# One of four low parts of each unit of the second expert table moves from VectorE to GpSimd, with four smaller edits

## The reference

```python
# 1. mixers: z = h @ w_in; windowed attention with sinks, gated; short convolution, gated; @ w_o; LN1
probs = softmax over a band of 128 keys and one sink          # 32 heads, 4 blocks of 128 tokens
h = layer_norm(ALPHA * h + mixed, ln1_g, ln1_b)
# 2. PEER: 8 heads x 16 chosen experts of 16384 for each token
u = take(u_tab, expert);  act = gelu(x . u);  wgt = gate * act
v = take(v_tab, expert);  y = sum over 128 slots of wgt * v
# 3. h = layer_norm(ALPHA * h + ffn, ln2_g, ln2_b)
```

## Time and profile before

| | us |
|---|---|
| median of 3 runs | 3801.84 (3796.93 to 3808.63) |
| the profiled execution's own time | 3810.41 |
| its span | 3808.6 |
| TensorE matmul busy | 3738.3 (98%) |
| VectorE busy | 2721.8 (71%) |
| ScalarE busy | 1394.6 (37%) |
| GpSimd busy | 1076.9 (28%) |

### The profile page before, as it was taken

One profiled execution on the slowest core, in us unless ns is written; L12 is line 12 of the kernel. 1 busy time (PEld: TensorE's weight loads), 2 busy tenths in 40 slices (PEclk: granted clock), 3 DMA queues, 4 the chain that ended last, 5 costly groups with the idle time before them and its releaser, 6 DMA issues.

```text
span 3808.6 us, 59840 instructions
## 1 busy us (share of the span) xinstructions
PE 3738.3 (98%) x24007; PEld 3431.3 (90%) x24007; DVE 2721.8 (71%) x3395; ACT 1394.6 (37%) x2023; POOL 1076.9 (28%) x579
## 2 busy tenths in 40 slices
PE   8999999999999999999999999999999999989998
PEld 8899999999977888888888899999999987878787
DVE  5644555456688765656556788888888877888888
ACT  5644444443425200000000144566665444434443
POOL 0000000000735433434444272232332212333432
PEclk9999999999999999999999999999999999999999
DMA  5345545554689999999999769999999989999996
GB/s 192 118 166 181 186 178 187 179 186 166 226 351 410 416 422 410 411 396 399 392 408 385 299 225 385 388 375 374 388 388 399 406 342 389 401 391 375 385 413 258
DMA packets 194970, 1232.67 MB, mean 324 GB/s; under 512 B 20144, under 2 KB 37120, under 8 KB 52736
## 3 DMA queue, kind: packets, MB, share of 16 engines
q1 hardware_dynamic: 109856, 656.51, 44.8%
q0 software_dynamic: 73728, 536.90, 34.6%
q10 hardware_dynamic: 11232, 37.23, 2.4%
HBM read 1193.34 MB, written 36.70 MB: 323 GB/s over the span
## 4 chain that ended last, share of the span: by engine, by line
PE 88%; DMA 5%; DVE 5%; ACT 1%; issue 1%; DVEq 0%; SPq 0%; ACTq 0%
PE dense_ps L1022 24%; PE dense_ps L1007 14%; PE dense_ps L1009 14%; PE dense_ps L1008 14%; PE dense_ps L1271 7%; PE score_ps L1271 4%; DMA wbuf<-in_peer_v_dram 3%; PE dense_ps L1050 3%; DMA wbuf<-in_w_units_dram 2%; PE oT_ps L1271 2%; PE o_ps L1271 2%; PE score_ps L1233 1%; PE score_ps L1123 1%; PE oT_ps L1163 1%; PE dense_ps L1145 1%
## 5 line engine op out<-in xcount | busy, mean ns | idle before, releaser
L1394 DVE TENSOR_TENSOR w_lo<-wbuf,w_hi_r 128x1024 fp32r<-128x1024 f32 x792 | 963.6, 1223 | 570.0 <-ACT w_hi_r L616 568.1
L616 ACT ACTIVATE w_hi_r<-wbuf 128x1024 fp32r<-128x1024 f32 x848 | 893.2, 1059 | 1118.6 <-PE dense_ps L1009 520.9
L1007 PE MATMUL dense_ps<-act_hi,w_hi_r 128*128 128x256 f32 x3968 | 1132.5, 285 | 3.1 <-DVE w_lo L1394 2.9
L1008 PE MATMUL dense_ps<-act_lo,w_hi_r 128*128 128x256 f32 x3968 | 1124.4, 283 | 0.0
L1009 PE MATMUL dense_ps<-act_hi,w_lo 128*128 128x256 f32 x3968 | 1124.2, 283 | 0.0
L1007 PEld LDWEIGHTS dense_ps<-act_hi,w_hi_r 128*128 128x128 f32 x3968 | 763.1, 192 | 15.4 <-issue 12.2
L1008 PEld LDWEIGHTS dense_ps<-act_lo,w_hi_r 128*128 128x128 f32 x3968 | 763.1, 192 | 0.0
L1009 PEld LDWEIGHTS dense_ps<-act_hi,w_lo 128*128 128x128 f32 x3968 | 762.8, 192 | 0.0
L1022 PE MATMUL dense_ps<-xT,wbuf 128*128 128x256 f32 x3136 | 687.2, 380 | 0.0
L1022 PEld LDWEIGHTS dense_ps<-xT,wbuf 128*128 128x128 f32 x3136 | 593.0, 190 | 91.0 <-issue 11.6
L562 POOL DMA_INDIRECT row<-in_peer_v_dram,expert x203 | 396.1, 1951 | 881.1 <-DVE h L1348 846.0
(11 more groups left out here) (292 smaller groups left out, 4294.9 us busy)
## 6 DMA issues: line engine op xcount, KB each, us to landing
wbuf<-in_w_units_dram SPq DMA_DIRECT2D x456, 1024.0 KB, 7.2
wbuf<-in_peer_v_dram SPq DMA_DIRECT2D x126, 1024.0 KB, 9.1
gate_spill<-gbuf ACTq DMA_DIRECT2D x8, 2048.0 KB, 12.0
e_gate<-gate_spill SPq DMA_DIRECT2D x32, 512.0 KB, 11.4
act_spill<-stage ACTq DMA_DIRECT2D x60, 256.0 KB, 9.2
e_act<-act_spill SPq DMA_DIRECT2D x30, 512.0 KB, 8.8
row<-in_peer_u_dram,expert POOLq DMA_INDIRECT x256, 14.2
row<-in_peer_v_dram,expert POOLq DMA_INDIRECT x203, 10.8
```

The costliest lines, as they stand in the source:

```text
L616: act.activation(hi_of(n)[j // 2][:, j % 2, :], w_of(n)[j // 2][:, j % 2, :], ACT.Copy).then_inc(w_hi_ready, 1)
L1007: nc.tensor.matmul(out, w[0], x[0], start=opens, stop=False)
L1008: nc.tensor.matmul(out, w[0], x[1], start=False, stop=False)
L1394: V.tensor_tensor(lo_of(n)[j // 2][:, j % 2, :], w_of(n)[j // 2][:, j % 2, :], hi_of(n)[j // 2][:, j % 2, :].bitcast(F32), ALU.subtract).t ...
```

## The change

It has five edits:

1. `by_pool` now also names quarter 1 of the units 4 to 59 of the V stage. So VectorE's list loses 56 low parts, and GpSimd's gets them. GpSimd's list for the V stage becomes a loop over units n: first all gathers with `FREE[g] <= ROWS_TO[n - 2]`, then `low(n, (1,))`.
2. In the U stage the gating of the one-hots comes before the high part (n+2, 2) rather than after it.
3. The weights of the final norm come in eight DMAs, of 512 columns each, over four pairs of units. For tile 0 the second step of the normalisation stays at unit 24 and the first goes to 23, the second residual split goes to 27, and the output is sent in four parts at units 26 to 29.
4. In half 1 the second group of five rows is spread: two ahead of the first softmax with the first five, one between `masks` and `denominators`, two after.
5. In half 0 the first `denominators` come ahead of the low parts (q0+2, 1) and (q0+2, 2).

```diff
-    return U_PQ < n < UNITS or UNITS + U_PQ + PLAIN_Q <= n < N_U + 4
+    return U_PQ < n < UNITS or UNITS + U_PQ + PLAIN_Q <= n < N_U + 4 or j == 1 and N_V + 4 <= n < N_V + 60
...
-            for g in range(ROWS_TO[N_U + 1] + 3, LATE_ROWS):
-                gather(g)
-            pool.wait_ge(dense_ready, N_V)
-            for g in range(LATE_ROWS, ALL_ROWS):
+            g = ROWS_TO[N_U + 1] + 3
+            for n in range(N_V + 4, N_V + 62):
+                while g < ALL_ROWS and FREE[g] <= ROWS_TO[n - 2]:
+                    if g == LATE_ROWS:
+                        pool.wait_ge(dense_ready, N_V)
+                    gather(g)
+                    g += 1
+                if n < N_V + 60:
+                    low(n, (1,))
+            for g in range(g, ALL_ROWS):
                 gather(g)
...
+                g = G_PER * (j + 1 - G_FIRST)
                 for k in range(3):
+                    if k == 2 and 0 <= g < HALF // 4:
+                        for r in range(G_PER):
+                            gate_rows(g + r)
                     split_hi(n + 2, k)
...
-STATS_AT, SD_AT, APPLY_AT, OUT_AT = (19, 61), (21, 61), (24, 62), (27, 62)
-RES_AT = (10, 24)
+STATS_AT, SD_AT, APPLY_AT = (19, 61), (21, 61), ((23, 24), (62, 62))
+OUT_AT = ((26, 27, 28, 29), (62, 62, 62, 62))
+RES_AT = (10, 27)
...
                 load(N_V + 2 + 2 * g)
                 load_e(3 + g)
+                if g == 0:
+                    sp.wait_ge(dense_ready, N_V)
+                load_ln2(0, g)
                 load(N_V + 3 + 2 * g)
-                if g % 2:
-                    sp.wait_ge(dense_ready, N_V)
-                    sp.dma_start(ln2[:, g // 2, :], ...).then_inc(ln2_in, 16)
+                load_ln2(1, g)
...
-                for n in range(n0, n0 + U_Q):
-                    rows(n)
+                rows(n0)
+                for p in range(2):
+                    rows(n0 + 1, p, 5)
...
                 masks(16 * b, 0, 0)
+                rows(n0 + 1, 2, 5)
+                denominators(16 * b)
+                for p in range(3, 5):
+                    rows(n0 + 1, p, 5)
                 split_lo(q0 + 2, 1)
                 split_lo(q0 + 2, 2)
-                denominators(16 * b)
```

More of the change, by code:

```diff
@@ L484, in load_act, with load_ln2 @@
                              act_spill[bass.ds(4 * i + q, 1), :, :].rearrange("o p x -> (o p) x")).then_inc(e_in[q % 2], 16)
+            def load_ln2(a, c):
+                part_c = slice(c * (D // 4), (c + 1) * (D // 4))
+                sp.dma_start(ln2[:, a, part_c], (ln2_b if a else ln2_g)[0, part_c].partition_broadcast(P)).then_inc(ln2_in, 16)
             def load_e(q, i=0):
@@ L511, in _ @@
                 load_e(3 + g)
+                if g == 0:
+                    sp.wait_ge(dense_ready, N_V)
+                load_ln2(0, g)
                 load(N_V + 3 + 2 * g)
-                if g % 2:
-                    sp.wait_ge(dense_ready, N_V)
-                    sp.dma_start(ln2[:, g // 2, :], (ln2_b if g // 2 else ln2_g)[0, :].partition_broadcast(P)).then_inc(ln2_in, 16)
+                load_ln2(1, g)
             with sp.Fori(0, GROUPS // 4 - 2) as i:
@@ L544, in _, with low @@
             pool.memset(mask[:, 0, 0:P], NEG).then_inc(masks_ok, 1)
-            def low(n):
-                for j in range(4):
+            def low(n, quarters=range(4)):
+                for j in quarters:
                     pool.wait_ge(w_hi_ready, HI[n, j])
@@ L633, in gathered_sd, with gathered_out @@
                 act.activation(sd2[:, :], mv2[:, 1:2], ACT.Sqrt, bias=eps[:, :]).then_inc(sd2_ready, 1)
-            def gathered_out(t):
+            def gathered_out(t, c):
+                part_c = slice(c * (D // 4), (c + 1) * (D // 4))
                 act.wait_ge(fin_step, 8 * (t + 1))
-                act.dma_start(out_v[:, t, :], h0[:, t, :]).then_inc(out_sent, 16)
+                act.dma_start(out_v[:, t, part_c], h0[:, t, part_c]).then_inc(out_sent, 16)
             def act_unit(j, placed=()):
@@ L948, in _ @@
                         gathered_sd(t)
-                    if m == OUT_AT[t]:
-                        gathered_out(t)
+                    for c in range(4):
+                        if m == OUT_AT[t][c]:
+                            gathered_out(t, c)
             for t in range(TILES):
@@ L958, in _ @@
                     act.dma_start(out_v[:, TILES + t, part_c], h1[:, t, part_c]).then_inc(out_sent, 16)
-            act.wait_ge(out_sent, 16 * (TILES + 2 * TILES))
+            act.wait_ge(out_sent, 16 * (4 * TILES + 2 * TILES))
         @block.tensor
@@ L1365, in finish_stats, with finish_apply @@
                 V.bn_aggr(mv2[:, :], bst2[:, :, :].rearrange("p c s -> p (c s)")).then_inc(fin_step, 1)
-            def finish_apply(t):
+            def finish_apply(t, second):
+                if second:
+                    dve.wait_ge(fin_step, 8 * t + 7)
+                    V.scalar_tensor_tensor(out=h0[:, t, :], in0=h0[:, t, :], scalar=rstd2[:, :], in1=ln2[:, 1, :],
+                                           op0=ALU.mult, op1=ALU.add).then_inc(fin_step, 1)
+                    return
                 dve.wait_ge(sd2_ready, t + 1)
@@ L1371, in finish_apply @@
                 dve.wait_ge(fin_step, 8 * t + 6)
-                dve.wait_ge(ln2_in, 32)
+                dve.wait_ge(ln2_in, 8 * 16)
                 V.scalar_tensor_tensor(out=h0[:, t, :], in0=h0[:, t, :], scalar=mv2[:, 0:1], in1=ln2[:, 0, :],
                                        op0=ALU.subtract, op1=ALU.mult).then_inc(fin_step, 1)
-                dve.wait_ge(fin_step, 8 * t + 7)
-                V.scalar_tensor_tensor(out=h0[:, t, :], in0=h0[:, t, :], scalar=rstd2[:, :], in1=ln2[:, 1, :],
-                                       op0=ALU.mult, op1=ALU.add).then_inc(fin_step, 1)
             for count in (masked, exp_done, pT_copied, aT_done, oT_ready, conv_step, gate_step, out_step,
@@ L1888, in _ @@
                         finish_stats(t)
-                    if m == APPLY_AT[t]:
-                        finish_apply(t)
+                    for second in range(2):
+                        if m == APPLY_AT[t][second]:
+                            finish_apply(t, second)
             for t in range(TILES):
```

## The result

| | before | after |
|---|---|---|
| median, us | 3799.39 (3796.90 to 3808.63, 4 runs) | 4059.05 (4051.01 to 4064.14, 4 runs) |
| ratio, 95% interval | | 1.0679 (1.0656 to 1.0703) |
| profiled execution, us | 3810.41 | 4061.67 |
| granted clock over the span | 0.992 | 0.969 |

The change makes the kernel 6.8% slower. The direction and the place were forecast; the size was not.

A forecast was written before the change was run, and what follows sets the result against it. TensorE, with matmuls in 98% of the span, was taken as the bound. 3810.4 + 407 (second table, units 5 to 59) + 3 (unit 7's gathers) - 18 (elsewhere) = 4202, stated as 4200; 8-in-10 range 4060 to 4255.

The forecast's parts named there:

- The chain: Second table: quarter 1 of unit n hangs through ScalarE, VectorE and GpSimd on quarter 2 of unit n-1; period 14.6 us.
- I take it that VectorE is first: Second table: VectorE's low part (n+1, 0) gets the ports before GpSimd's low part; period 18.9 us with the clock's loss.
- U + 11.34: End of GpSimd's low part if VectorE is first; U is when TensorE ends quarter 2 of unit n-1.
- the 2.24 that remain after VectorE's end: Earlier trace at 949.64: GpSimd's low part ended 2.24 us after VectorE's; taken to show reads later than its start.
- and through a series if there is no pause: GpSimd waits through VectorE's unbroken series; so held through low part (n+1, 0) and `e_mult` or `e_rest` to U + 9.10.
- The clock: Second table: TensorE returns at half clock after longer waits, losing 1.75 to 2.41, mean 2.1 us a unit, in quarter 1.
- the clock doesn't fall: Rival, regular waits in the second table: 4087 with VectorE first, 3966 with GpSimd first; chance 0.1 in its two forms.
- the 3.75 worked out for GpSimd first: TensorE's least wait ahead of quarter 1 in every unit: part ready at U + 9.19, needed at U + 5.44.
- The gains outside: Outside the second table: one-hots -9.2, first softmaxes -3.9 and -2.0, some 3 us of clock; -18 us.
- the right rival: GpSimd gets the ports first in the second table: period 16.7 us, +286, 4082; chance 0.2.
- Not slower: Rival, second table: gathers ahead don't wait for the last row; 3760 at best, some 3780 with DMA waits; chance 0.07.
- what would show it: Signs: one 5 to 6 us TensorE wait per unit before quarter 1, half clock behind each, DMA well under 0.98.

The follow-up runs named there:

- Taking it out by one index: Changed kernel with ROWS_TO[n - 3] for ROWS_TO[n - 2], so GpSimd's low part goes ahead of gathers waiting for section n-2: 3792.83 us, ratio 0.9984.
- shortening it by 1.08: Changed kernel with GpSimd making only the first 512 of 1024 columns of each moved low part, VectorE the rest: 3962.82 us, ratio 1.0420.
- the kernel with the rows early: Changed kernel with VectorE's rows of a second-table section put ahead of low part (n+2, 2) instead of after it: 3863.08 us, ratio 1.0159.
- the kernel with the pause: Changed kernel with a one-column memset on GpSimd, and a wait for it, between gathers and each moved low part: 4111.21 us, ratio 1.0819.
- an added wait: Changed kernel with GpSimd's low part of unit n waiting until VectorE has made low part (n+1, 0): 4212.85 us, ratio 1.1082.
- with the low part first: Changed kernel with each GpSimd low part ahead of the gathers that wait for section n-2, by ROWS_TO[n - 3]: 3792.83 us, ratio 0.9984.
- with quarter 3: Changed kernel with quarter 3 instead of quarter 1 on GpSimd, gathers still ahead of it: 3857.59 us, ratio 1.0162.
- without the move: Changed kernel with edit 1 undone, edits 2 to 5 kept: 3770.06 us, ratio 0.9937; once more 3769.56 us, ratio 0.9926.
- the kernel with the move alone: Kernel before with edit 1 alone: 4072.42 us, ratio 1.0729.
- half width: Changed kernel with GpSimd making 512 of the 1024 columns of each moved low part, VectorE the other 512: 3962.82 us, ratio 1.0420.

## Why the forecast was right, and where it failed

**The chain** was right. Each of its steps stands in one unit of the trace to 0.02 us up to GpSimd's start. Taking it out by one index gave back 266 of 289 us, shortening it by 1.08 gave back 96 (46 in waits and 45 in the clock, by its block), and taking the row from behind low part (n+2, 2) gave back 196, as expected.

**The step that failed** is the one put as "its first reads come later than its start, ... I take it that VectorE is first". It put GpSimd's low part at U + 11.34, and it ended at U + 9.10; that is 2.2 us a unit, the 121 us between 4202 and 4081. GpSimd was ahead of VectorE's low part (n+1, 0) in 53 of 55 units, in 46 of them against an earlier stamp. The rows behind that choice were of two kinds that don't bear on it: the earlier trace rows, where GpSimd's low part had no gather ahead of it, and the 2.24 that remain after VectorE's end. The stamps of the two starts were 0.01 to 0.04 apart in the 46, and they don't decide directly behind a gather: GpSimd then won even where VectorE's stamp was 0.17 earlier, and up to 0.60 earlier in the kernel with the rows early, and lost with a pause of 0.19. That the gather by itself keeps VectorE out is a rival that the traces speak against: 488 of VectorE's low parts, `e_mult` and `e_rest` started in the last 0.60 us of a gather with no low part within 0.5 us behind it, over all thirteen traces, and none took more than 0.01 over its 1.22. 

The Trainium skill, SBUF — State Buffer, section "Who interferes with whom", gives the shared ports to whichever instruction is issued first, for its whole length. The whole length agrees (3.46 for 1.22); which one was issued first can't be told from the start stamps here.

**A second step** in the same price was wrong, and hidden by the first: "and through a series if there is no pause". GpSimd's low part in the kernel with the pause waited for one instruction of VectorE, not two. Had VectorE been first, as I took it, the period would by that kernel have been some 17.5 (4111 us), not 18.9. Neither order of the two came near 4200; an added wait did (4213). It is not that two never pass: behind a row they did, 7 times with the low part first and 5 times with quarter 3.

**The clock** was forecast at 2.1 us a unit. In the block the matmuls are busy 707.8 us against 604.5 without the move: 103.3, by 55 that is 1.88. It isn't the same in each unit: among the three shown one keeps 1.00 and takes 14.77, which is the chain alone (forecast 14.6), one takes 16.37 at 0.90, one 17.25 at 0.80. The rival "the clock doesn't fall" is true of some units only (8 of 54 from wait to wait).

**The wait** of 3.67 us in the mean (201.7 by 55) is near the 3.75 worked out for GpSimd first: 10.88 + 3.67 + 1.88 = 16.4 of the 16.60.

**The gains outside** were forecast at 18 and are 27.1. The two first softmaxes gave 3.9 and 5.8 of it, about the waits and the clock behind them. The one-hots gave the larger part: 17.0 in the first table's stretch, of which 9.3 is idle time, the 9.2 forecast. The other 7.7 are the same matmuls in less busy time. I had 3 us of clock for all places together. Not all of the 17.0 is the edit's: the kernel with the move alone, which lacks it, is 3.6 quicker there than the kernel before. What is left is small and not the edits': 1.6 us in the first 24 us of the kernel and 1.3 near 940, less 2.6 lost near 1040. The same code was up to 1.5 slower in the first of these places in other runs, and six other runs with edit 4 lose nothing in the last.

**The sum** for the right rival was 3810.4 + 286 + 3 - 18 = 4081; the profiled execution took 4061.7. The difference of 20 is the block (923 forecast with unit 7's gathers, 912.9 measured) and the gains outside (9.1).

**Not slower** was wrong for the reason given: the gather ahead of the low part does wait for the last row. But its sums of 3760 to 3780, what edits 2 to 5 give with VectorE in time, were what the kernel without the move showed, 3770. Even with no chain (3793) moving the low parts cost 23 us: VectorE needed no help. It is the version without the move that beats both kernels.

Of "what would show it": idle once a unit released by `w_lo`, the gather 0.26 behind the row, DMA at 0.73 and the one-hot waits gone were right; 5 to 6 us a wait and half clock behind each were wrong, and GpSimd's low part at 2.35 said which engine was first.

What stays open: why the start stamps mislead directly behind a gather (the low part acts as if it had asked for the ports 0.60 to 0.64 us before its stamp, an estimate from the cases below), when one instruction of VectorE passes it and when two, and why the clock falls in some units and not in others with the same wait.

## What to carry to other kernels

Before moving work to an engine with spare time, read what stands ahead of it in that engine's list and what that waits for. A helper behind a wait on the bottleneck's own last step makes a loop, and its cost comes again in every unit; one index in the list was worth 266 us here. And where two engines exclude each other and a forecast hangs on which is first, price both orders and the number of instructions that each one really passes, rather than choose by start stamps a few hundredths apart.

## What the runs showed of the hardware

- GpSimd's low part 0.01 to 0.02 us behind a gather's end was ahead of all 208 VectorE instructions (206 low parts, one row, one residual split) whose stamp was 0.01 to 0.60 us earlier, and behind all 72 whose stamp was 0.64 to 1.03 us earlier, over the eight kernels with such places. With a pause of 0.19 or more behind the gather it lost to a start 0.04 earlier (3.43 instead of 2.41) and once to one 0.01 later (3.49).
- GpSimd's low part was mostly held by one VectorE instruction and got in ahead of the next, also where that followed without a pause: in 41 of 55 with the added wait, with a row next, and in 46 of 55 with the pause. It was passed by two in 7 of 54 with the low part first and in 5 of 55 with quarter 3, each time by a row and then a low part.
- A gather is not let in like that: 5.08 and 7.28 us for 1.68, ending 0.80 after the end of a whole series of VectorE's instructions. It holds none of them in its own last 0.60 us (488 cases, none longer by more than 0.01).
- A wait 0.8 us shorter (half width) won 1.66 us a unit, as TensorE kept its clock from wait to wait in 23 of 54 cases instead of 8.
